# Row copies, closing steps and a query set apart over the first round of a token tile

## The reference, cut to what matters

```python
def peer_ffn(xn, w_q, sub_keys, u_tab, v_tab):
    q = (xt @ w_q).reshape(n_tok, PEER_HEADS, 2, PEER_DHALF)      # 8 heads
    scores = einsum('thcd,ckd->thck', q, sub_keys)                # 2 x 128 keys
    top_s, top_i = lax.top_k(scores, 16)
    ...                                       # 16 x 16 sums, top 16 of them
    act = gelu(einsum('td,tkd->tk', xb, u_tab[eb]))               # 128 experts a token
    return einsum('tk,tkd->td', gb * act, v_tab[eb])
```

## Time and profile before

| | us |
|---|---|
| median of 3 runs | 3154.34 |
| lowest, highest | 3153.10, 3156.09 |
| the profiled execution | 3158.17 |
| its span in the profile | 3156.4 |
| VectorE busy | 2199.8 (70%) |
| TensorE matmul busy | 2147.1 (68%) |
| ScalarE busy | 1549.0 (49%) |
| GpSimd busy | 1155.9 (37%) |
| DMA of the gathers, share of 16 engines | 83.0% |
| mean granted TensorE clock | 0.781 |

### The profile page before, as it was taken

One profiled execution on the slowest core, in us unless ns is written; L12 is line 12 of the kernel. 1 busy time (PEld: TensorE's weight loads), 2 busy tenths in 40 slices (PEclk: granted clock), 3 DMA queues, 4 the chain that ended last, 5 costly groups with the idle time before them and its releaser, 6 DMA issues.

```text
span 3156.4 us, 40113 instructions
## 1 busy us (share of the span) xinstructions
PE 2147.1 (68%) x13768; PEld 1281.2 (41%) x13768; DVE 2199.8 (70%) x6053; ACT 1549.0 (49%) x3986; POOL 1155.9 (37%) x1041
## 2 busy tenths in 40 slices
PE   7878788674457798777855799878675655453334
PEld 6776454340024475555523466545442312120001
DVE  8646888857776777767676657777866666667663
ACT  3514556443334766775433476787543423343332
POOL 0012344334443333434343433433445444334441
PEclk8889888785567899998876799999886866565555
DMA  6228999999999999979999999998999999999995
GB/s 212 67 86 334 419 419 417 396 369 421 421 420 364 419 404 391 403 287 410 419 420 414 377 356 399 384 388 339 421 420 420 420 421 421 421 419 421 421 421 241
DMA packets 182413, 1185.36 MB, mean 376 GB/s; under 512 B 19648, under 2 KB 25792, under 8 KB 50880
## 3 DMA queue, kind: packets, MB, share of 16 engines
q0 software_dynamic: 147456, 1073.81, 83.0%
q1 hardware_dynamic: 34752, 108.98, 9.1%
HBM read 1180.61 MB, written 2.10 MB: 375 GB/s over the span
## 4 chain that ended last, share of the span: by engine, by line
DMA 37%; PE 31%; ACT 16%; DVE 9%; issue 5%; POOL 2%; another core or an unknown queue 1%; ACTq 0%; SPq 0%; POOLq 0%; DVEq 0%
DMA arena<-uv_tab,cols 37%; PE ps L760 7%; PE xps L696 7%; DVE arena L2179 4%; PE ps L696 4%; POOL arena L653 2%; ACT L1415 2%; ACT scr L1427 2%; ACT cols L1420 2%; PE ps L735 2%; PE xps L1118 2%; PE xps L1192 1%; ACT cols L1415 1%; PE xps L1169 1%; PE xps L1189 1%
## 5 line engine op out<-in xcount | busy, mean ns | idle before, releaser
L653 POOL DMA_INDIRECT arena<-uv_tab,cols x1024 | 1151.7, 1125 | 1944.8 <-PE ps L760 1372.2
L2179 DVE CUSTOM_DVE_ANT_0 arena<-arena 128x1024 f32<-128x1024 f32 x1024 | 1249.8, 1222 | 588.6 <-DMA arena<-uv_tab,cols 558.5
L760 PE MATMUL ps<-arena,scr 128*32 128x512 f32 x4096 | 743.3, 806 | 751.8 <-ACT scr L1427 729.2
L1415 ACT ACTIVATE cols<-cols 128x2 f32<-128x2 f32 x512 | 105.2, 206 | 1008.1 <-DVE cols L2179 998.0
L760 PEld LDWEIGHTS ps<-arena,scr 128*32 128x32 f32 x4096 | 92.7, 123 | 1121.8 <-ACT scr L1427 1036.8
L696 PE MATMUL xps<-arena,wring 128*128 128x256 f32 x1600 | 393.6, 396 | 15.8 <-ACT arena L1628 8.3
L696 PEld LDWEIGHTS xps<-arena,wring 128*128 128x128 f32 x1600 | 304.1, 197 | 105.8 <-issue 43.1
L1427 ACT ACTIVATE scr<-sel,cols 128x32 f32<-128x32 f32 x1024 | 275.3, 316 | 48.4 <-ACT cols L1420 1.9
L696 PE MATMUL ps<-arena,wring 128*128 128x256 f32 x1152 | 292.2, 411 | 6.6 <-DVE arena L1807 4.1
L696 PEld LDWEIGHTS ps<-arena,wring 128*128 128x128 f32 x1152 | 233.7, 207 | 90.7 <-issue 46.2
L1420 ACT ACTIVATE cols<-cols 128x1 f32<-128x1 f32 x1024 | 247.9, 289 | 20.5
(11 more groups left out here) (447 smaller groups left out, 2911.9 us busy)
## 6 DMA issues: line engine op xcount, KB each, us to landing
wring<-wall SPq DMA_DIRECT2D x176, 512.0 KB
arena<-uv_tab,cols POOLq DMA_INDIRECT x1024
arena<-wall SPq DMA_DIRECT2D x16, 512.0 KB, 7.5
h<-xT SPq DMA_DIRECT2D x2, 1024.0 KB, 11.3
arena<-glu_w SPq DMA_DIRECT2D x2, 1024.0 KB, 12.7
out<-arena SPq DMA_DIRECT2D x4, 512.0 KB, 21.0
arena<-s_b SPq DMA_DIRECT2D x1, 512.0 KB, 9.1
arena<-s_bt SPq DMA_DIRECT2D x1, 512.0 KB, 9.8
```

Source lines behind the costliest of these rows:

```text
L653: pool.indirect_dma_start(out=whole_row(at), out_offset=None, in_=uv_tab, in_offset=bass.IndirectOffsetOnAxis(ap=ids[g % 2][:, k:k + 1], a ...
L760: mm = pe.matmul(ps[4 + half][32 * c:32 * c + 32, :], wdiag[:, b % PAIRS, j, :], pair_row(at + j, 1)[:, T * half:T * half + T], start=(g % ...
L1415: mark(act.activation(gelu[g % 2][:, 2 * b:2 * b + 2], dots[g % 2][:, 2 * b:2 * b + 2], ACT.Gelu))
L2179: dve.tensor_tensor_reduce(u, u, xrep[:, block_of(k), :], 1.0, 0.0, ALU.mult, ALU.add, dots[g % 2][:, k:k + 1]).then_inc(s["dot_done"], 1)
```

## The change

Slots, half slots and the order in which the lists hold things are changed, and the first tile's rows get banks of their own:

- In a tile's first round, row copy 5 goes from slot 1 to 2, copy 6 from 1.5 to 3.5, copy 7 from 2 to 5. The closing steps go from 2.5, 3, 4.5 to 6, 7, 8.5 (ScalarE: from 3, 3.5, 5 to 6.5, 7.5, 9), and the norm of `tile_done` from slots 6 to 9 to slots 10 to 13.
- The query of rounds 16, 32 and 48 goes from slot 5 to 9, its scores so from 9.5 to 13.5, and `route` of every eighth round starts at slot 14 in place of 11. The softmax of the round after goes from slot 3 to 5.
- The first tile's row copies leave `side`: new functions `first_tile_rows` use `ps[0]` and `ps[1]` in turn. TensorE does six of them ahead of `across(0)` (before: two) and two behind the second scores. ScalarE copies four before the softmax (before: two), four after the second scores. Dots of round 0 wait for these copies by a new semaphore; `u_rows(1)`, the next user of the banks, waits for all eight.
- `first_apply(1)` comes behind dot 1 of round 0 on VectorE, not behind dot 0.

```diff
 def query_at(gi, q):
-    return 16 * r + (8 if r == 0 else 5 if r % 8 == 0 and r > 0 else 2)
+    return 16 * r + (8 if r == 0 else 9 if r % 8 == 0 and r > 0 else 2)
 def rows_at(t, i):
-    return TOPK * PH * t + (-7, -5.5, -4, -2.5, 0.5, 1, 1.5, 2)[i]
+    return TOPK * PH * t + (-7, -5.5, -4, -2.5, 0.5, 2, 3.5, 5)[i]
 def side_order():
-    todo = [(-10, "q", 0, -1), (-9, "sc", 0, -1), (-8, "q", 0, -2), (-7.5, "x", 0, 0), (-7.2, "x", 0, 1), (-7, "sc", 0, -2)]
-    todo += [(-6 + 0.1 * i, "x", 0, i) for i in range(2, 8)] + [(4.5, "q", 0, 0), (6.7, "sc", 0, 0)]
+    todo = [(-10, "q", 0, -1), (-9, "sc", 0, -1), (-8, "q", 0, -2), (-7, "sc", 0, -2), (4.5, "q", 0, 0), (6.7, "sc", 0, 0)]
...
-        todo += [(TOPK * (PH * t + 8) + (2.5, 3, 4.5)[i], "hy", t, i) for i in range(3)]
+        todo += [(TOPK * (PH * t + 8) + (6, 7, 8.5)[i], "hy", t, i) for i in range(3)]
@@ TensorE
+            def first_tile_rows(i):
+                pe.wait_ge(s["xn_first"], 1)
+                if i >= 2:
+                    pe.wait_ge(s["rows_done"], i - 1)
+                for k in range(4):
+                    for e in range(4):
+                        mm = pe.matmul(ps[i % 2][32 * e:32 * e + 32, tl(k)], xn[:, 4 * (i % 2) + k, 32 * (i // 2):32 * (i // 2) + 32],
+                                       ident[:, :], start=True, stop=True, skip_group_check=True)
+                mm.then_inc(s["rows_mm"], 1)
...
+                    if g and i == 0:
+                        pe.wait_ge(s["rows_done"], 8)
...
-            for i in range(2):
-                to_rows(0, i)
+            for i in range(6):
+                first_tile_rows(i)
             across(0)
             first_scores(1)
-            for i in range(2, 8):
-                to_rows(0, i)
+            for i in range(6, 8):
+                first_tile_rows(i)
             first_sum(1)
...
-                    if k in (2.5, 3, 4.5) and done is not None:
-                        finish(done, (2.5, 3, 4.5).index(k))
+                    if k in (6, 7, 8.5) and done is not None:
+                        finish(done, (6, 7, 8.5).index(k))
@@ ScalarE
+            def first_tile_rows(i):
+                act.wait_ge(s["rows_mm"], i + 1)
+                act.activation(xrep[:, i // 2, T * (i % 2):T * (i % 2) + T], ps[i % 2][:, :],
+                               ACT.Copy).then_inc(s["rows_done"], 1)
...
-            for i in range(2):
-                to_rows(0, i)
+            for i in range(4):
+                first_tile_rows(i)
             soft(0)
             first_scores(1)
-            for i in range(2, 8):
-                to_rows(0, i)
+            for i in range(4, 8):
+                first_tile_rows(i)
             first_norm(1)
...
-                    if k == 3 and r + 1 < ROUNDS:
+                    if k == (5 if r % PH == 1 else 3) and r + 1 < ROUNDS:
                         soft(r + 1)
...
-                    if k in (3, 3.5, 5) and done is not None:
-                        finish(done, (3, 3.5, 5).index(k))
+                    if k in (6.5, 7.5, 9) and done is not None:
+                        finish(done, (6.5, 7.5, 9).index(k))
@@ VectorE
-                if g % PH == 0 and k % 8 < 2:
+                if g == 0 and k % 8 < 2:
+                    dve.wait_ge(s["rows_done"], 2 * block_of(k) + 2)
+                elif g % PH == 0 and k % 8 < 2:
                     dve.wait_ge(s["side_done"], SIDE["x", g // PH, 2 * block_of(k) + 1] + 1)
...
             def tile_done(t):
-                yield 6
+                yield 10
...
-                        yield 7 + i
+                        yield 11 + i
...
-                    if r == 0 and k == 0:
+                    if r == 0 and k == 1:
                         first_apply(1)
...
-                    if k == (14 if r == 0 else 11 if r % PH == 0 else ROUTE_SLOT):
+                    if k == (14 if r % PH == 0 else ROUTE_SLOT):
                         nxt = route(r + 2) if r + 2 < ROUNDS else iter(())
```

More of the change, by code:

```diff
@@ L531, in trunk @@
             "g_sq", "g_sum", "g_root", "mix1_ready", "out_added", "hsq_ready", "hsum", "h_root", "xn_ready",
-            "first_w", "first_mm", "xn_first", "q_first",
+            "first_w", "first_mm", "xn_first", "q_first", "rows_mm", "rows_done",
             "q_mm", "m_mm", "o_mm", "side_mm", "side_done", "na_ready",
@@ L723, in scores @@
                 mm.then_inc(s["side_mm"], 1)
+            def first_tile_rows(i):
[7 more added lines that the diff above has]
+                mm.then_inc(s["rows_mm"], 1)
             def to_rows(t, i):
                 side_free(("x", t, i))
-                if t == 0:
-                    pe.wait_ge(s["xn_first"], 1)
-                else:
-                    pe.wait_ge(s["xn_ready"], t // 2 + 1)
+                pe.wait_ge(s["xn_ready"], t // 2 + 1)
                 at = P * (t % 2) + 32 * (i // 2)
@@ L1396, in scores @@
                 m.then_inc(s["side_done"], 1)
+            def first_tile_rows(i):
+                act.wait_ge(s["rows_mm"], i + 1)
+                act.activation(xrep[:, i // 2, T * (i % 2):T * (i % 2) + T], ps[i % 2][:, :],
+                               ACT.Copy).then_inc(s["rows_done"], 1)
             def to_rows(t, i):
                 act.wait_ge(s["side_mm"], SIDE_MM["x", t, i])
[L1401 to L1402 removed]
+                act.wait_ge(s["dot_done"], PH * TOPK * t - TOPK + 8 * (i // 4) + 7 + i // 2 % 2)
                 act.activation(xrep[:, i // 2, T * (i % 2):T * (i % 2) + T], side[:, :],
```

2 lines of the change are left out of this document (removed).

## The result

The changed kernel took 3129.64 us, the median of 4 runs (3125.44 to 3131.06), against 3155.22 for the kernel before (4 runs, 3153.10 to 3158.18): a ratio of 0.9916, with a 95% interval of 0.9899 to 0.9933, or 25.6 us less. The forecast was 42 us less, 3113, in a range of 3094 to 3138. The sign and the range held; the size was too large by 16 us in this measurement, which lies outside the 12 us around 3113 that the prediction gave its main case. One of the four runs of the changed kernel's third measurement, further down, took 4911.34 us and is left out of every figure. The profiled execution took 3128.93 with a span of 3127.2.

What follows compares the result with a forecast made beforehand. The prediction held the kernel bound by the rate at which expert rows arrive, so only holes in the stream could be won: 11.5 + 26.5 + 6 - 2 = 42 us less, forecast 3113 us, range 3094 to 3138.

Steps and rivals of the forecast that it cites:

- main case: Whole kernel: the summed gain of 42 us, a time within 12 us of 3113; chance 0.48.
- rival A: Tile boundaries: spread pieces run at half clock, half the light rounds' term and no heavy rounds' term remain; 3132, chance 0.18.
- Start, forecast 11.5: First tile: two banks speed the row copies, the second tile's norm and gather 8 come earlier; 8.9 to 14.8 us.
- half of the stalls: Start: of ScalarE's remote waits, 7.2 us beyond what TensorE explains, half was taken to return, giving the term 11.5.
- Rival B: Start: remote waits return whole or longer, first gather 1.35 us later; term 3 instead of 11.5, time 3121, chance 0.12.
- Rounds 16 and 32, forecast 9.5 and 6.5: Tiles' first rounds: spread pieces cut the lag between value pairs from 16.6 us to 3 or so.
- Round 8, forecast 10.5: First round of a tile: spread pieces and the S5 gate's Gelu ahead of the closing root win 10.5 us.
- Rounds 24 and 40, forecast +6: Heavy first rounds, TensorE busy 56.09 of 63 us and 50.28 of 57: at most 13.6 us won, at least 5 lost.
- Routing, -2: Rounds after every eighth: seven routing steps bunched at slot 5 cost 0 to 4.1 us in each of five short-ring rounds.
- Rival D: Seven rounds (9, 17, ... 57): bunched routing makes ids late and gathers wait, 29 us; slower, at 3174, chance 0.07.
- The norm behind the second dot, 0: Start, VectorE: moving the norm costs nothing, as dot 1 takes 1.2 us and its row lands long before the root.
- The signs that were named: GpSimd start wait 13 to 19 us; rounds 8, 16, 32 at 390 GB/s or more; round 24 at 290 to 330.

Runs made afterwards that it cites:

- third measurement: The changed kernel without any edit, measured again on the first chip: 3120.48 us (3 runs), ratio 0.9883 to the kernel before.
- second measurement: The changed kernel without any edit, measured again on another chip: 3109.24 us, ratio 0.9898 to the kernel before.
- second execution: The kernel before, without any edit, profiled again on the first chip: 3153.91 us.
- The one experiment aimed at the cause: Against the changed kernel, GpSimd holds its third gather until all eight row copies of the first tile are done: 3112.43 us, ratio 0.9904.

## Why the prediction was right or wrong

- **The sign, and that the gain is holes: right.** Three measurements of the change give 25.6, 32.7 and 37.3 us against a forecast of 42. All are below the forecast, so the sum was too high by 5 to 16 us. The first of them, 3129.64, lies outside the main case (3101 to 3125) and next to the 3132 of rival A, whose mechanism did not occur (below); only the range, made wide for the rivals, holds it.
- **Start, forecast 11.5 (8.9 to 14.8): mechanism right, and the term depends on the chip.** Where ScalarE's remote waits stand, the hole went from 18.7 to 9.3 and 8.3, so 9.4 to 10.4 less; on the other chip the changed kernel has 2.8. No kernel of before was profiled there, so what the edit gave on that chip is not known from a trace. The step that failed is "half of the stalls": on the first chip they come back whole and on the other they don't come at all. Rival B had the first of these conditions, but its price, a term of 3 in place of 11.5, was too dark: with the waits whole the start still gave 9.4 to 10.4. The price in the ids was less than taken: the rows followed each other at 0.92 us, not 1.1, and relative to the query's end the first gather is later by some 0.5 us rather than 1.35.
- **Rounds 16 and 32, forecast 9.5 and 6.5: right.** They gave 10.1 and 7.4, and rounds 17 to 19 took 2.0 back, 4.2 and 2.7 in the other two measurements, which the prediction hadn't. What these rounds pay isn't traced further. The lag between value pairs shrank to 2.6 us (17.5 less 14.9), forecast 3 or so. Not every step was under 4.98, though: that with the last row copy and the first closing step took 7.42.
- **Round 8, forecast 10.5: wrong.** It gave 6.2, less 2.7 in round 9. The step was "with the closing root at slot 9 the Gelu at 5 comes first": true, but the gate's Sigmoids come later than slot 5, and the closing steps fell among them: the root's Ln and Exp between the two Sigmoids (4.60 us), the first two steps between TensorE's matmuls for the gate. A piece moved out of one knot was set into the next. The experiment with the closing at 9, 10 and 11.5 shows it by taking VectorE's wait away (9.73 in the result, 9.0 on its own chip).
- **Rounds 24 and 40, forecast +6: size fair, reason wrong.** They gave 5.0 + 3.0, less 2.8 in round 25. The prediction read 56.09 busy of 63 as a TensorE with no room. Taking 3.8 us of that work out moved nothing in round 24, and 2.3 us in round 40: a high busy share of an engine that stands in a chain of waits doesn't make its work the bound. What does bound round 24 is open.
- **Routing, -2: not borne out.** GpSimd waits for ids before no round from 1 to 46, and with the old slots rounds 9 and 25 pay the same. Rival D's condition, ids later than the fifth value pair, did not occur.
- **The norm behind the second dot, 0: right in size, by luck in the reason.** Dot 1 was to be done "long before the root". Where ScalarE stalls it is (228.13 against 236.23). Without the stalls the root is ready at 227.46 and the norm starts at 229.42, behind dot 1; with the norm behind dot 0 it starts at 227.86. That costs nothing because the first eight gathers are still arriving.
- **Rival A, pieces among waits at the half clock:** not borne out. It left half of the light rounds' term and none of the heavy rounds'; they gave 23.7 and 8.0. The clock itself tells nothing here: the mean granted clock of round 16, between the half clock of 1.2 GHz and the full 2.4, is 0.85 in the changed kernel, but 0.76 in one execution of the kernel before and 0.89 in the other. The rule cited from the Trainium skill (TensorE: Matmul & The Clock Gate, "HAM oscillation") is by these rows neither confirmed nor contradicted.
- **The signs that were named:** GpSimd's start wait within 13 to 19 (17.73), round 24 within 290 to 330 GB/s (319) and round 16's longest wait under 7 held, as did 390 GB/s in rounds 16 and 32, not in round 8 (364). The first gather was to come near 219.5 and came at 217.50 in the first trace, where all before it was 1.16 us early, and at 219.04 and 219.83 in the second and third. One sign of being wrong came as well: on the first chip the remote waits stand ahead of the second tile's root (229.21, the root's Exp at 235.88), and the start still gave most of its term. Of the others only a trace: VectorE waits once for scores, 0.8 us, in the third measurement.

In sum, for the result: start 9.4, rounds 8, 16 and 32 23.7, rounds 24 and 40 8.0, together 41.1 gross against 44 forecast. Given back in rounds 9, 17 to 19 and 25: 7.5, which stood nowhere in the sum. Of the 5.1 that are still missing to 28.5, most lie in rounds 6 and 7 (0.9 before, 3.7 after) and 20 and 21 (8.7, 11.9), which the change doesn't touch; the second measurement has 1.8 and 8.1 there, the third 0.8 and 11.6, the kernel before in its second execution 0.8 and 7.1. So rounds 6 and 7 are the spread of one execution, and rounds 20 and 21 may be more than that. That a stream held up less at one place meets the next wait sooner is the plainest reading of the 7.5; for rounds 9 and 25 the experiments tie it to the later closing steps or the norm behind them, for 17 to 19 it is only argued.

## What to carry to other kernels

Before a piece of work is moved away from a knot, list on every engine that it uses what will stand around it at the new place, functions of ScalarE's tables among them: two chains with different functions that interleave pay a table load at each change (1.28 us each, three of them here). To learn whether a busy engine is the bound of a stage, take some of its work out and look, for its busy share doesn't say. And set aside part of the local gains, here a fifth (7.5 of 41.1), for the waits right behind them.

## What the runs showed of the hardware that was not expected

**TensorE sticks, nearly always at narrow matmuls, on one chip and not on the other.** In the changed kernel's start TensorE transposes the last two rows, 64 matmuls, 32 to a row. In the result's execution, the timeline of TensorE:

```profile
218.67 1.99 PE L731 MATMUL xps<-ident,arena 128*32 128x128 f32 x51 [1.05 <-ACT arena L1410]
221.01 0.44 PE L731 MATMUL xps<-ident,arena 128*32 128x128 f32 x5 [0.35 <-issue]
221.78 0.43 PE L731 MATMUL xps<-ident,arena 128*32 128x128 f32 x4 [0.33 <-issue]
223.24 0.39 PE L731 MATMUL xps<-ident,arena 128*32 128x128 f32 x3 [1.03 <-issue]
223.98 0.27 PE L731 MATMUL xps<-ident,arena 128*32 128x128 f32 x1 [0.35 <-issue]
```

and on the other chip:

```profile
220.20 1.95 PE L731 MATMUL xps<-ident,arena 128*32 128x128 f32 x64 [1.05 <-ACT arena L1410]
```

In the first, the matmuls stop after 51 and then come in driblets with nothing to wait for; ScalarE gets the first of the two rows at 223.29, though its 32 matmuls are among the first 51, and the second at 229.21, though the last matmul began at 223.98. These are ScalarE's two remote waits. In the five other executions with this start on the first chip the stop comes after 51 matmuls four times and after 52 once. The sums of such waits over a whole execution, of the changed kernel:

```profile
ACT arena L1417 <- remote: 57.8, 19, 7.9
ACT arena L1410 <- remote: 9.6, 2, 5.3
...
PE ps L767 <- issue: 34.8, 16, 5.1
PE ps L742 <- issue: 8.6, 4, 4.2
```

The value pairs (L767) stick too; they and the row copies are matmuls of 32 columns. A single stop of 2.3 us stands at a closing step's full-width ones (L780). The kernel before has 37.3 us in 11 remote waits and 22.0 in 9 stops at its value pairs. On the other chip four kernels with the same matmuls show not one of either, and there the kernel before took 3141.97 us against 3153.73 and 3157.76 on the first, the changed one 3109.24 against 3120.48. The difference between the chips is 12 to 16 us for the kernel before, and 11 for the changed one. For the start the trace shows what the stops cost (a hole of 8.3 to 9.3 against 2.8); that they make the rest of the difference is likely and not shown.

The cause is open. That the stop comes after 51 or 52 matmuls in six executions speaks for something tied to the place in the program; but the prediction's thought, instruction fetch (the rule it cited from the Trainium skill, Runtime: NRT & Kernel Launch, "Instruction fetch mechanics"), gets no support: an instruction queue brings a block of 16 KB between 216 and 217 in the result's execution and between 218 and 219 in that of the other chip, in both less than a microsecond before the first gather and with no further one for the next ten. The one experiment aimed at the cause ran where there were no stops.

**Two chips, two times, one gain as far as can be told.** The same two kernels differ by 25.6 and 37.3 us in two measurements with the waits and by 32.7 on the chip without, each with an interval of 5 to 8 us to either side. Below about 5 us nothing here is settled by the time alone; the holes tell more.
